# State-space recurrence of a hybrid decoder step: TensorE adds the turned products, the scans read PSUM banks, and GpSimd computes the samples' states

## The reference, cut to what matters

```
s[t] = a * s[t-1] + Bu[t]          # complex a, s, Bu;  t = 0..255 for the prompt, s[-1] = 0
y[t] = Re(C s[t]) + D u[t]         # then gelu, a gated linear unit, the output projection
# the 8 sample requests: the same recurrence over 4 positions from a cached state
```

## Time and profile before

| what | value |
|---|---|
| median of 3 runs | 2285.87 us (2283.56 to 2285.88) |
| the profiled execution's own time | 2286.42 us |
| span of that execution, first to last instruction | 2284.7 us |
| the stretch with the recurrence, from the samples' first product to `quarter_ready` 4 | 1252.6 to 1354.8 us |

### The profile page before, as it was taken

The page is one execution under the profiler, slowest core; times in us unless marked ns, Lnnn a source line. Parts: engine busy times, 40 slices in busy tenths (PEclk is TensorE's granted clock), DMA queues, the critical chain, the costliest instruction groups (busy, mean ns, idle before and its releaser), DMA issues.

```text
span 2284.7 us, 38224 instructions
## 1 busy us (share of the span) xinstructions
PE 1959.6 (86%) x14225; PEld 1483.7 (65%) x14225; DVE 1198.9 (52%) x3489; ACT 649.8 (28%) x977; POOL 983.8 (43%) x840
## 2 busy tenths in 40 slices
PE   9788899999999667899888568999999997666676
PEld 4565799999998333344357234999999995333332
DVE  2454499723334443488546962899233333443433
ACT  1332244455554000121124111344555550000000
POOL 0111358860001576677611301579710005777774
PEclk9799999999999889999997679999999998999988
DMA  6465424445545999999931234144554448999998
GB/s 241 148 246 185 157 77 164 154 160 166 166 166 185 346 374 395 401 392 386 371 137 54 70 114 155 67 155 151 166 162 164 165 165 296 410 409 409 410 409 328
DMA packets 177961, 529.89 MB, mean 232 GB/s; under 512 B 22034, under 2 KB 48178, under 8 KB 177394
## 3 DMA queue, kind: packets, MB, share of 16 engines
q0 software_dynamic: 87296, 310.68, 35.5%
q1 hardware_dynamic: 89330, 216.25, 28.1%
q10 hardware_dynamic: 1152, 0.52, 0.1%
HBM read 524.69 MB, written 2.69 MB: 231 GB/s over the span
## 4 chain that ended last, share of the span: by engine, by line
PE 60%; DMA 15%; POOL 10%; DVE 8%; issue 4%; ACT 2%; SPq 0%; DVEq 0%; ACTq 0%; POOLq 0%
PE bank L903 11%; PE bank L905 11%; PE bank L904 11%; DMA v_slot<-in_peer_v,v_rows 10%; PE bank L726 9%; PE bank L967 5%; POOL v_slot L670 4%; DMA v_slot_of_columns<-in_peer_v,v_rows 4%; POOL u_low L661 3%; PE bank L1045 3%; POOL v_slot_of_columns L670 2%; PE bank L985 2%; PE bank L943 1%; PE bank L962 1%; PE bank L849 1%
## 5 line engine op out<-in xcount | busy, mean ns | idle before, releaser
L670 POOL DMA_INDIRECT v_slot<-in_peer_v,v_rows x417 | 394.7, 946 | 623.5 <-PE bank L905 441.1
L903 PE MATMUL bank<-h_parts,u_high 128*128 128x288 f32 x2048 | 607.0, 296 | 7.2 <-POOL u_low L661 5.5
L904 PE MATMUL bank<-h_parts,u_high 128*128 128x288 f32 x2048 | 604.4, 295 | 0.0
L905 PE MATMUL bank<-h_parts,u_low 128*128 128x288 f32 x2048 | 602.8, 294 | 0.0
L903 PEld LDWEIGHTS bank<-h_parts,u_high 128*128 128x128 f32 x2048 | 384.1, 188 | 11.0 <-POOL u_low L661 9.0
L905 PEld LDWEIGHTS bank<-h_parts,u_low 128*128 128x128 f32 x2048 | 385.7, 188 | 0.0
L904 PEld LDWEIGHTS bank<-h_parts,u_high 128*128 128x128 f32 x2048 | 384.5, 188 | 0.0
L1505 ACT CAST u_high<-u_slot 128x1024 fp32r<-128x1024 f32 x256 | 268.8, 1050 | 399.8 <-PE bank L905 241.8
L661 POOL TENSOR_TENSOR u_low<-u_slot,u_high 128x1024 fp32r<-128x1024 f32 x120 | 320.2, 2678 | 93.8 <-ACT u_high L1505 93.8
L967 PE MATMUL bank<-v_slot_of_columns,weight_columns 128*32 128x512 f32 x636 | 221.3, 671 | 106.5 <-DMA v_slot<-in_peer_v,v_rows 79.0
L2042 DVE TENSOR_TENSOR u_low<-u_slot,u_high 128x1024 fp32r<-128x1024 f32 x136 | 166.7, 1226 | 276.9 <-ACT u_high L1505 276.9
(11 more groups left out here) (373 smaller groups left out, 2427.9 us busy)
## 6 DMA issues: line engine op xcount, KB each, us to landing
u_slot<-in_peer_ut SPq DMA_DIRECT2D x256, 512.0 KB, 3.5
w_q<-in_peer_w_q SPq DMA_DIRECT2D x8, 2048.0 KB, 16.3
region<-in_cache_a_kt SPq DMA_DIRECT2D x8, 960.0 KB, 11.9
region<-in_cache_a_v SPq DMA_DIRECT2D x8, 960.0 KB, 11.4
v_slot<-in_peer_v,v_rows POOLq DMA_INDIRECT x417, 8.4
region<-in_ev_w_in SPq DMA_DIRECT2D x3, 2048.0 KB, 15.6
region<-in_pool_kv POOLq DMA_DIRECT2D x40, 128.0 KB, 5.1
region<-in_ev_w_out SPq DMA_DIRECT2D x2, 2048.0 KB, 10.5
```

Source lines behind the costliest of these rows:

```text
L670: pool.indirect_dma_start(out=VS[l][slot], out_offset=None, in_=v_rows, in_offset=bass.IndirectOffsetOnAxis(ap=IDX[:, at:at + 1], axis=0)) ...
L903: pe.matmul(bank, uh, HR[:, 0, c, :], start=(c == 0), stop=False)
L904: pe.matmul(bank, uh, HR[:, 1, c, :], start=False, stop=False)
L905: ins = pe.matmul(bank, ul, HR[:, 0, c, :], start=False, stop=(c == KC - 1))
```

## The change

Per quarter, VectorE now makes only the four products of the turn (`states_products`): cos*re and cos*im into `XR2`, sin*im and -sin*re in place into `BU[g]`. TensorE adds them in pairs (`turned_sums`): for each part and half quarter two matmuls of 128 x 512 with the identity, accumulated in a PSUM bank of VectorE's four. The scans take their input from these banks, two scans to a bank, and free it. The samples' recurrence moves to GpSimd's queue, behind its 16 key pages and ahead of its wait for `sd_scores`. The orders on TensorE and VectorE are rewritten: the products run one quarter ahead of the scans in the first half, and on TensorE `states_in(2)` follows `latent_scores(0)`, `latent_out_turn(0)` follows `turned_sums(1)`, and `states_out(2)` precedes `latent_values(1)`.

```diff
+            def sample_states():
+                pool.wait_ge(sem("s5_factors_made"), 3)
+                pool.wait_ge(sem("tbls_then_odd_small_loaded"), 48 + 16 * 16)
+                pool.wait_ge(sem("bu_ready"), 20)
+                by = [bc(S5P[:, 11], 2, DEC_B), bc(S5P[:, 12], 2, DEC_B)]
+                prev = [S0[:, k] for k in range(2)]
+                for n in range(DEC_T):
+                    now = [BUS[:, k, :, n:NS:DEC_T] for k in range(2)]
+                    tm = [STMP[:, k] for k in range(4)]
+                    pool_step(pool.tensor_tensor(tm[0], by[0], prev[0], ALU.mult))
...
+                    pool_settle()
+                    pool_step(pool.tensor_tensor(now[0], now[0], tm[0], ALU.add))
+                    pool_step(pool.tensor_tensor(now[1], now[1], tm[1], ALU.add))
+                    pool_settle()
...
+                pool_settle()
+                pool.nop().then_inc(sem("samples_ready"), 1)
@@ GpSimd's queue
                 for b in (2, 3):
                     pages_of(pool, CKPT[b], I["pool_ckv"][:, :, 0:P], b, "latents_loaded_by_pool0")
+                sample_states()
 
                 pool.wait_ge(sem("sd_scores"), 1)
@@ TensorE
+                def turned_sums(g):
+                    pe.wait_ge(sem("products_ready"), g + 1)
+                    for k in range(2):
+                        parts = (XR2[g % 2][k], BU[g][:, 1 - k])
+                        for h in range(2):
+                            bank = to_dve()
+                            for n, part in enumerate(parts):
+                                ins = pe.matmul(bank[:, :].rearrange("p (q n) -> p q n", n=SEQ), ident, part[:, 2 * h:2 * h + 2, :],
+                                                start=(n == 0), stop=(n == 1))
+                            ins.then_inc(d_full, 1)
+
                 latent_scores(0)
+                states_in(2)
                 sample_states_out()
+                turned_sums(0)
                 latent_turn(0)
                 latent_values(0)
+                turned_sums(1)
+                latent_out_turn(0)
                 states_out(0)
                 states_in(3)
-                latent_out_turn(0)
+                turned_sums(2)
                 states_out(1)
                 latent_scores(1)
+                turned_sums(3)
                 latent_turn(1)
+                states_out(2)
                 latent_values(1)
-                states_out(2)
                 latent_out_turn(1)
                 states_out(3)
@@ VectorE
-                def states_turn(g):
+                def states_products(g):
                     dve.wait_ge(sem("bu_ready"), 8 * (g + 1) + 4 * (g // 2))
-                    cmul(XR2[g % 2], turns_of(g), [BU[g][:, k] for k in range(2)], T12, conj=True)
+                    cos, sin = turns_of(g)
+                    re, im = BU[g][:, 0], BU[g][:, 1]
+                    out = XR2[g % 2]
+                    step(dve.tensor_tensor(out[0], cos, re, ALU.mult))
+                    step(dve.tensor_tensor(out[1], cos, im, ALU.mult))
+                    settle()
+                    step(dve.tensor_tensor(im, sin, im, ALU.mult))
+                    step(dve.scalar_tensor_tensor(out=re, in0=sin, scalar=-1.0, in1=re, op0=ALU.mult, op1=ALU.mult))
+                    settle()
+                    say("products_ready")
 
                 def states_scan(g):
                     for k in range(2):
-                        for q in range(4):
...
+                        for h in range(2):
+                            bank = full()
+                            for q in (2 * h, 2 * h + 1):
...
+                            settle()
+                            free()
@@ VectorE's queue
                 absorbed_queries()
-                sample_states()
...
                 latent_scores(0)
+                states_products(0)
                 out_of_sample_states()
-                states_turn(0)
+                states_products(1)
                 states_scan(0)
+                latent_out(0)
                 states_turn_back(0)
-                states_turn(1)
-                latent_out(0)
+                states_scan(1)
+                latent_out_turned(0)
                 out_of_states(0)
-                states_scan(1)
+                states_products(2)
                 states_turn_back(1)
-                latent_out_turned(0)
-                states_turn(2)
+                states_scan(2)
                 out_of_states(1)
-                states_scan(2)
+                latent_scores(1)
+                states_products(3)
                 states_turn_back(2)
-                latent_scores(1)
-                states_turn(3)
                 states_scan(3)
+                out_of_states(2)
                 latent_out(1)
-                out_of_states(2)
                 states_turn_back(3)
                 latent_out_turned(1)
                 out_of_states(3)
```

More of the change, by code:

```diff
@@ L650, in _, with pool_step, pool_settle @@
             v_rows = I["peer_v"].rearrange("l a b d -> (l a b) d")
+            nstep = [0]
+            def pool_step(ins):
+                nstep[0] += 1
+                ins.then_inc(sem("pool_step"), 1)
+            def pool_settle():
+                pool.wait_ge(sem("pool_step"), nstep[0])
+            def sample_states():
[8 more added lines that the diff above has]
+                    pool_step(pool.tensor_tensor(tm[0], by[0], prev[0], ALU.mult))
+                    pool_step(pool.tensor_tensor(tm[1], by[0], prev[1], ALU.mult))
+                    pool_step(pool.tensor_tensor(tm[2], by[1], prev[1], ALU.mult))
+                    pool_step(pool.tensor_tensor(tm[3], by[1], prev[0], ALU.mult))
+                    pool_settle()
+                    pool_step(pool.tensor_tensor(now[0], now[0], tm[0], ALU.add))
+                    pool_step(pool.tensor_tensor(now[1], now[1], tm[1], ALU.add))
+                    pool_settle()
+                    pool_step(pool.tensor_tensor(now[0], now[0], tm[2], ALU.subtract))
+                    pool_step(pool.tensor_tensor(now[1], now[1], tm[3], ALU.add))
+                    pool_settle()
+                    prev = now
+                for k in range(2):
+                    pool_step(pool.tensor_copy(LASTS[:, k], BUS[:, k, :, DEC_T - 1:NS:DEC_T]))
+                pool_settle()
+                pool.nop().then_inc(sem("samples_ready"), 1)
             def peer(l):
@@ L1309, in odd @@
                     turn_tokens(lambda c: O1[:, t, c * P:c * P + P], t, P, 0, 4, to_act)
-                states_in(2)
                 def states_out(g):
@@ L2395, in states_turn_back @@
                     say("quarter_ready")
-                def sample_states():
-                    dve.wait_ge(sem("bu_ready"), 4)
-                    ab = [bc(par[11], 2, DEC_B), bc(par[12], 2, DEC_B)]
-                    prev = [S0[:, k] for k in range(2)]
-                    for n in range(DEC_T):
-                        now = [BUS[:, k, :, n:NS:DEC_T] for k in range(2)]
-                        tm = [STMP[:, k] for k in range(4)]
-                        cmul([tm[0], tm[1]], ab, prev, [tm[2], tm[3]])
-                        for k in range(2):
-                            TT(now[k], now[k], tm[k], ALU.add)
-                        prev = now
-                    for k in range(2):
-                        step(dve.tensor_copy(LASTS[:, k], BUS[:, k, :, DEC_T - 1:NS:DEC_T]))
-                    settle()
-                    say("samples_ready")
                 def out_of_states(g):
```

6 lines of the change are left out of this document (3 added, 3 removed).

## The result

The changed kernel takes 2289.86 us (median of 8 runs, 2287.74 to 2294.75); the kernel before takes 2285.32 beside it (8 runs, 2280.43 to 2286.13). The ratio is 1.0034 [1.0022, 1.0046]: slower by 4.5 us, 0.2%. 2288.3 had been forecast, and 2283 to 2297 as range.

The account below looks back on a forecast made before the run. VectorE was taken as the bound; pages 6.0 us earlier, 7.9 given back in a TensorE-bound tail, 0.5 for bank releases: +2.4 us, 2288.8, or 2288.3 after taking off the profiled run's 0.55 above the median; range 2283 to 2297.

Parts of the forecast that it names:

- GpSimd's price: Samples' recurrence on GpSimd: 34 x 0.5 us plus 13 waits of 0.15, ready at about 1262, hidden.
- The rival of a late GpSimd: At 0.8 us per instruction TensorE waits for the samples' states: +7.4 us, 2293.3; chance 0.25.
- the contention: VectorE and GpSimd both reading SBUF as `states_products(0)` starts: some four instructions at 0.5 us each touched, scores not.
- The limit of 0.64 us per instruction: GpSimd's samples stay hidden up to some 0.64 us per instruction (21.7 / 34); beyond it the late GpSimd decides.
- The first half: Round 0's scores to quarter 1's turn back: scores end at 1261.4, ten earlier; `quarter_ready` 2 at 1303.1, 6.0 us earlier.
- quarter 0's sums: Eight matmuls of `turned_sums(0)` on TensorE: 8.9 us with low clock, taken as 8.4 for a short pause, to 1274.7.
- The page queue: SyncE's pages before round 1: 32 end at 1304.2, twelve key pages and landing take 15.1 us; scores start 1319.3, 6.0 earlier.
- The tail: End of round 1's scores on VectorE to last C matmuls: TensorE the path, 33.8 us for 25.9, 7.9 given back.
- last matmuls with C: Last group of the tail on TensorE, behind quarter 3's turn back: 6.1 us.
- The rival on the other side: TensorE at 2.4 GHz wherever needed, 5.9 us less in scores, sums and last C matmuls: -3.5, 2282.4; chance 0.12.
- The half microsecond for the banks' releases: Releases of the scans' banks in four quarters, half of it exposed: 0.5 us added to the loss.

Follow-up runs that it names:

- e7: Changed kernel with round 1's key pages 4 and 6 asked for behind `quarter_ready` 1, the value pages behind them; ratio to the kernel before 1.0001.
- e8: Changed kernel with quarter 3 turned by VectorE, quarter 2's turn back ahead of round 1's scores, and round 1's pages reordered; ratio to the kernel before 0.9951.
- e12: Kernel before with only the samples' recurrence moved to GpSimd and round 1's pages reordered; VectorE turns every quarter; ratio to the kernel before 0.9989.
- e5: Kernel before, unchanged, run again on the same chip as e6; ratio to the kernel before 1.0017.
- e1: Kernel before with only the samples' recurrence moved to GpSimd; turn, scans and orders as before; ratio to the kernel before 0.9983.
- e3: Changed kernel with quarter 3 turned by VectorE and scanned from SBUF, quarter 2's turn back ahead of round 1's scores; ratio to the kernel before 1.0004.
- e11: The same kernel as e3, run again; ratio to the kernel before 0.9989.
- e6: Changed kernel, unchanged, run again on the same chip as e5; ratio to the kernel before 1.0030.
- e4: Changed kernel with quarter 3's eight sums on TensorE made twice into the same banks; ratio to the kernel before 1.0064.
- e9: Changed kernel with added identity matmuls keeping TensorE busy in its pauses ahead of four groups; ratio to the kernel before 0.9990.

## Why the prediction was right, point by point

The forecast of +2.4 us came out as +4.5, within its own range and with the mechanism named: earlier pages, and a tail in which TensorE is the path. But it had a difference too small to be told from none, and the measured one is nearly twice as large and clear of noise; by the stretch it is +5.2. From the stretch's start, in us:

| mark | before | forecast | measured |
|---|---|---|---|
| round 0's scores reduced | 19.1 | 9.05 | 9.1 |
| `quarter_ready` 2 | 56.8 | 50.8 | 53.0 |
| round 1's scores begin | 72.9 | 67.0 | 69.3 |
| tail | 26.0 | 33.8 | 34.7 |

- *GpSimd's price.* 34 x 0.5 us taken, 16.4 us in all measured, waits included (0.40 to 0.53 each). It was hidden. The rival of a late GpSimd is refuted, and the contention that the text had confined to a few instructions could not arise: GpSimd was done at 1254.89, before the products, which read two SBUF tensors, began at 1257.08. (The limit of 0.64 us per instruction is 0.62 by the prediction's own terms.)
- *The first half.* Right to 0.1 us for round 0's scores. Behind them the sum was 2.3 us short. Most of it is quarter 0's sums: they took 9.9 us, where the prediction had put 8.4 because of the short pause (2.55 us) before them, and they began at a clock of 0.5 all the same. Another 0.3 lies in the turn and the values. The last 0.5 lies in quarter 0's matmuls with C, which wait for a bank that the scans of quarter 1 free, and eight scans from banks take 5.50 us where 4.8 had been taken.
- *The page queue.* From `quarter_ready` 2 to the scores' start it is 16.3 us (1300.8 to 1317.06), and it was 16.2 before (1309.1 to 1325.30). The prediction's 15.1 ends at the landing, leaves out the 1.08 us of "issue" behind it, and yet compares its result with 1325.30: this makes the gain 1.1 us too large. The prediction also said that SyncE would issue without a gap. It did not: 16 value pages ended 1.3 us before `quarter_ready` 2, which sets the rest alone. By luck this gives the 1.1 us back: the prediction had counted the twelve pages from 1304.2, 1.1 us behind its `quarter_ready` 2, and in truth they follow `quarter_ready` 2 at once. So the gain up to the scores is short by the 2.3 us of the first half alone. With fewer key pages behind that wait the scores start 5 to 6 us earlier (e7, e8, e12).
- *The tail.* Forecast 33.8, measured 34.7: the sums 9.03 for 8.9, the turn of the probabilities 1.0, the values 2.2, each as written. The term that was mis-sized is the last matmuls with C, 7.06 for 6.1. The pause before them is not longer than before's (4.72 against 5.53 us); the clock stays at 0.50 for the first 4.7 us, where before's rose after 3.1. The other traces have the same group at 6.1 (e5) and 7.2 us (e1, e12) behind 5.5 us of pause, and at 6.1 (e3), 6.4 (e11) and 7.1 (e6, e7) behind 4.7. So this term is uncertain by 1 us from run to run; what decides when the clock rises is not shown. e4 confirms that the tail is TensorE's, e3 that 9 us of it go with `turned_sums(3)` and the place of quarter 2's turn back.
- *The rival on the other side,* TensorE at 2.4 GHz everywhere, was priced at 5.9 us less; e9 made that state in the three groups named and gave 5.7. The nearness is in part luck: the last matmuls gained 2.4 us, not 1.5, and 0.9 were lost again to the added matmuls. What kept it from happening is what the text named: the pauses for pages and for the products.
- *The halves.* The prediction had a gain of 6.0 up to round 1's scores and a loss of 7.9 behind. Measured: 3.4 to 3.7 and 8.7. The half microsecond for the banks' releases was tested by no run of its own. (The chances, added up, are 0.09 for faster and 0.53 for the same, where the text has 0.10 and 0.52.)

## What to carry to other kernels

Work moved from a busy engine to an idle one pays only where the busy one is the path all the way; before a stage's end, ask what the two engines do by turns. Here the sums on TensorE, with the orders that go with them, gained 3.7 us of stretch in quarters 0 to 2; in quarter 3, where TensorE was the path, every added matmul landed on the end (e4: 6.9 us for eight), and the tail was 9 us longer. When an engine gets faster, the next bound is often a queue with a fixed order. Here eight key pages asked for earlier in each of two queues took some 8 us from the changed kernel's stretch, more than the change had added, but only 0.3 us where VectorE was the path (e12). And a pause on TensorE can cost twice, itself and the half-speed start of the group behind it: sized by e9, 1.9 to 2.4 us for each group of this tail. Before such a gain is read from one trace, look at where the clock rose: that alone moved the stretch of one kernel by more than 2 us.

## What the runs showed of the hardware that was not expected

- GpSimd's 128 x 128 products and sums (strided outputs among them) take 0.40 to 0.53 us, where a 128 x 1024 subtraction took 2.32: 4.4 to 5.8 times for eight times the elements.
- A scan of 128 x 256 costs 0.63 us when it reads a PSUM bank (rows of two, 1.26 us, in the changed kernel's quarter 2) and 0.60 from SBUF (eight in 4.77). The wait and the release for each pair cost more than the bank: eight scans take 5.50 us with them, 0.69 each.
- Pauses of 1.56 and 1.61 us ahead of round 1's scores (e7, e8) left TensorE's clock at full; those of 2.14, 2.55 and 7.86 us ahead of the changed kernel's sums ended at 0.5. Added matmuls in the pause gave 1.00 at the group's start (e9). Behind like pauses the low clock did not always last as long: see the last matmuls with C above.
- One chip to another: the same kernel takes 2282 to 2285 us on two chips and 2364 to 2369 on two others, 3.5 to 3.8% more, while the stretch looked at here takes 108.4 and 108.7. In the two traces of the kernel before, 38 us of the difference lie ahead of the stretch and 44 behind it; what they are was not looked into.
